# A hybrid decoder step on one core: the second token group's queries without their norm, routes among the dots, kept weights, and other last groups

## The reference

```python
h = h + merged @ w_out                                   # after three gated branches
x = _rmsnorm(h, norm2_g)                                 # h * rsqrt(mean(h*h) + 1e-6) * g
q = (x @ w_q).reshape(t, 8, 2, 128)                      # 8 product-key heads
s = einsum('thpc,pkc->thpk', q, sub_keys)                # scores against 2 x 128 keys
sv, si = top_k(s, 16); cand = sv[..0..] + sv[..1..]      # 256 candidates of a head
cv, ci = top_k(cand, 16); experts = i1 * 128 + i2        # 16 of 16384 experts
act = gelu(einsum('thkd,td->thk', u_tab[experts], x))    # dots with the first table
h = h + einsum('thk,thkd->td', softmax(cv) * act, v_tab[experts])
y = _rmsnorm(h, final_norm_g)
```

## Time and profile before

| | |
|---|---|
| median of three runs | 1943.35 us (1941.68 to 1944.21) |
| profiled execution | 1947.41 us, of it span 1945.6 us |
| PE, DVE, ACT, POOL busy | 86%, 71%, 27%, 34% |
| granted TensorE clock, mean | 0.949 |
| DMA | 675.14 MB, of which 577.23 MB are gathers |

### The profile page before, as it was taken

How to read it: one execution, slowest core, us unless ns; L and a number is a source line. 1 busy time by engine, 2 the same in 40 slices (tenths; PEclk the granted TensorE clock), 3 DMA queues, 4 the chain that set the end, 5 groups by cost and what they waited for, 6 DMA issues and landing times.

```text
span 1945.6 us, 17733 instructions
## 1 busy us (share of the span) xinstructions
PE 1674.4 (86%) x5411; PEld 999.5 (51%) x5411; DVE 1388.4 (71%) x3407; ACT 521.7 (27%) x1203; POOL 663.9 (34%) x605
## 2 busy tenths in 40 slices
PE   8999999999888999998868999877777777787876
PEld 7888987887555555554434555323333212333332
DVE  5998684227788777777787778776777776777754
ACT  3121142113333433332222223332222122321221
POOL 0020030002434343333434344444444453445441
PEclk9999999999999999999979999998999898989898
DMA  5452465548999999999989999999999999999995
GB/s 209 141 87 98 154 146 164 176 150 339 418 400 412 419 418 418 418 419 401 419 349 413 419 420 414 421 422 410 414 419 413 412 416 419 408 414 415 421 412 245
DMA packets 112687, 675.14 MB, mean 347 GB/s; under 512 B 12784, under 2 KB 15296, under 8 KB 42576
## 3 DMA queue, kind: packets, MB, share of 16 engines
q0 software_dynamic: 80816, 577.23, 73.0%
q1 hardware_dynamic: 31216, 95.87, 14.3%
q10 hardware_dynamic: 560, 0.92, 0.2%
HBM read 665.79 MB, written 6.21 MB: 345 GB/s over the span
## 4 chain that ended last, share of the span: by engine, by line
PE 46%; DMA 36%; issue 8%; DVE 6%; POOL 2%; ACT 2%; ACTq 0%; DVEq 0%; POOLq 0%
DMA upper<-in_peer_uv,upper 20%; PE pair L1157 19%; DMA lower<-in_peer_uv,upper 16%; PE pair L667 7%; PE pair L678 6%; PE pair L1024 4%; DVE upper L2080 2%; PE pair L781 2%; ACT upper L1550 1%; PE pair L972 1%; POOL upper L643 1%; DVE lower L2080 1%; POOL lower L643 1%; PE pair L793 1%; PE pair L712 1%
## 5 line engine op out<-in xcount | busy, mean ns | idle before, releaser
L1157 PE MATMUL pair<-upper 128*128 128x512 f32 (+1 forms) x1144 | 570.4, 641 | 152.6 <-ACT upper L1550 152.3
L643 POOL DMA_INDIRECT upper<-in_peer_uv,upper x324 | 369.2, 1139 | 500.6 <-PE pair L1157 437.4
L1157 PE MATMUL pair<-lower,upper 128*128 128x512 f32 (+1 forms) x772 | 382.1, 637 | 93.7 <-ACT upper L1550 93.6
L1157 PEld LDWEIGHTS pair<-upper 128*128 128x128 f32 (+1 forms) x1144 | 218.5, 198 | 434.0 <-issue 276.0
L643 POOL DMA_INDIRECT lower<-in_peer_uv,upper x220 | 255.2, 1160 | 483.0 <-PE pair L1157 305.0
L2080 DVE CUSTOM_DVE_ANT_0 upper<-upper 128x1024 f32<-128x1024 f32 x172 | 210.7, 1225 | 122.4 <-DMA upper<-in_peer_uv,upper 122.1
L1157 PEld LDWEIGHTS pair<-lower,upper 128*128 128x128 f32 (+1 forms) x772 | 148.0, 198 | 283.5 <-issue 185.5
L2080 DVE CUSTOM_DVE_ANT_0 upper<-upper,lower 128x1024 f32<-128x1024 f32 x152 | 185.8, 1222 | 87.6 <-DMA upper<-in_peer_uv,upper 86.7
L1550 ACT ACTIVATE upper<-upper 128x128 f32<-128x128 f32 (+1 forms) x479 | 159.9, 386 | 308.3 <-DVE upper L2096 308.1
L2080 DVE CUSTOM_DVE_ANT_0 lower<-lower,upper 128x1024 f32<-128x1024 f32 x116 | 142.1, 1225 | 85.5 <-DMA lower<-in_peer_uv,upper 85.5
L1024 PE MATMUL pair<-lower 128*128 128x288 f32 x704 | 194.0, 413 | 2.6 <-ACT upper L1420 2.6
(11 more groups left out here) (420 smaller groups left out, 1760.6 us busy)
## 6 DMA issues: line engine op xcount, KB each, us to landing
lower<-in_w_in SPq DMA_DIRECT2D x64, 512.0 KB, 7.0
lower<-in_peer_q SPq DMA_DIRECT2D x32, 512.0 KB, 7.9
lower<-in_proj SPq DMA_DIRECT2D x48, 256.0 KB, 7.1
lower<-in_w_out SPq DMA_DIRECT2D x16, 512.0 KB, 6.0
upper<-in_peer_uv,upper POOLq DMA_INDIRECT x324, 11.8
upper<-in_cache_k SPq DMA_DIRECT2D x8, 512.0 KB, 4.5
upper<-in_cache_v SPq DMA_DIRECT2D x8, 512.0 KB, 3.7
lower<-in_peer_uv,upper POOLq DMA_INDIRECT x220, 11.8
```

The costliest lines, as they stand in the source:

```text
L643: pool.indirect_dma_start(row(g), None, a["peer_uv"], bass.IndirectOffsetOnAxis(ap=idx[:, n % 8, j:j + 1], axis=0)).then_inc(row_in[g % RI ...
L1157: mm = pe.matmul(pairs[n % 2][0:rows, h, :], diag[:, (nth - 1) % DIAGS, 0:rows], row(g)[:, D + h * 512:D + (h + 1) * 512], start=(j == min ...
```

## The change

Five edits. (1) The second group's `xbT_b` is h g2 without the norm's factor, written by DVE behind each w job. The sums of squares are taken as columns (job sq, 24 narrow matmuls), and the factor `rcol_b` (three columns) multiplies the scores in ACT's copies out of PSUM and the argument of the gelu. The queries of head 0 start before the sums, and the transposes of h are split around them; empty slots are 4 + 4 in place of 15 + 6. (2) Route 1 is no longer ahead of the first dot: routes 1 and 2 run in job 0, five steps behind each dot from the fifth on. ACT's exponentials follow. (3) Three heads' first parts, in place of four, are ahead of the loop. (4) The query weights of heads 1 and 2 (four blocks of 512 KB) get a place of their own in the memory of ring places 8 and 9, are loaded once the trunk no longer needs it, and gathers 8 and 9 wait until they have been used. (5) The last job's groups are 4, 4, 2 and six single rows, in place of 4, 4, 4 and four single ones; the residual is added in PSUM before row 13, in place of row 12.

```diff
-EARLY_HEADS = 4
+EARLY_HEADS = 3
...
-BANK_JOBS += [("gapm", 8)] + [(f"w{_j}", KD) for _j in range(KD)] + [("gap0", 15), ("ssb", KD)]
-for _t in range(2, 5):
-    BANK_JOBS += [(f"ht{_t}.{_b}", 4) for _b in range(2)] + [(f"gaph{_t}", 2)]
-BANK_JOBS += [("q0.0", KD), ("q0.1", KD)] + [(f"xt{_t}.{_b}", 4) for _t in range(2, 5) for _b in range(2)]
+BANK_JOBS += [("gapm", 8)] + [(f"w{_j}", KD) for _j in range(KD)] + [("gap0", 4)]
+BANK_JOBS += [(f"ht{_t}.0", 4) for _t in range(2, 5)] + [("q0.0", KD), ("q0.1", KD), ("sq", KD)]
+BANK_JOBS += [(f"ht{_t}.1", 4) for _t in range(2, 5)] + [("gaph", 4)]
+BANK_JOBS += [(f"xt{_t}.{_b}", 4) for _t in range(2, 5) for _b in range(2)]
...
+KEPT = ["Aq1.0", "Aq1.1", "Aq2.0", "Aq2.1"]
...
-    last = [range(12, 16)] if n < NJ - 1 else [range(j, j + 1) for j in range(12, 16)]
-    return [range(0, 4), range(4, 8), range(8, 12)] + last
+    ends = (4, 8, 12, 16) if n < NJ - 1 else (4, 8, 10, 11, 12, 13, 14, 15, 16)
+    return [range(lo, hi) for lo, hi in zip((0,) + ends, ends)]
...
+        kept_w = at(33024, 4, 1024)
...
+            def kept_loads():
+
+                sp.wait_ge(lnx_ok, 2 * HALF - 1)
+                for i in range(4):
+                    sp.dma_start(kept_w[:, i, :], a["peer_q"][2 + i]).then_inc(kept_in[i], 16)
+
             for h in range(PH):
+                if h == 1:
+                    kept_loads()
                 for b in range(2):
-                    late_load(f"Aq{h}.{b}", a["peer_q"][2 * h + b])
+                    if f"Aq{h}.{b}" not in KEPT:
+                        late_load(f"Aq{h}.{b}", a["peer_q"][2 * h + b])
...
+                if g in (8, 9):
+                    bank_filled(pool, f"Aq{g - 7}.1")
...
+            def late_squares():
+
+                ps = begin_bank("sq")
+                pe.wait_ge(h2sqb_ok, KD)
+                n = 0
+                for t in range(3):
+                    for k in range(KD):
+                        mm = pe.matmul(ps[:, 4 * t:4 * t + 4], h2sq_b[:, k, t * P:(t + 1) * P], ones[:, 0:4],
+                                       start=(k == 0), stop=(k == KD - 1))
...
-                for _ in range(15):
+                for _ in range(4):
                     yield
-                ps = begin_bank("ssb")
-                for k in range(KD):
-                    pe.wait_ge(h2sqb_ok, k + 1)
-                    mm = pe.matmul(ps[:, 0:REST], ones, h2sq_b[:, k, :], start=(k == 0), stop=(k == KD - 1))
...
+                for t in range(2, 5):
+                    yield from turned(f"ht{t}.0", h2T_b, t, P if t < TILES else NB * NT, 4)
+                for b in range(2):
+                    yield from dense_query(0, b)
+                yield from late_squares()
+                for t in range(2, 5):
+                    yield from turned(f"ht{t}.1", h2T_b, t, P if t < TILES else NB * NT, KD)
...
-                    if n == NJ - 1 and j == 12:
+                    if n == NJ - 1 and j == 13:
...
-                               scale=rcol[:, t:t + 1] if t < 2 else 1.0).then_inc(gel_ok, 1)
+                               scale=rcol[:, t:t + 1] if t < 2 else rcol_b[:, t - 2:t - 1]).then_inc(gel_ok, 1)
...
+            act.wait_ge(rcol_ok, 3)
+            exp_of(0)
             first_query(1)
-            for h in range(1, EARLY_HEADS):
-                first_query(h + 1)
-                if h == 1:
-                    act.wait_ge(rcol_ok, 3)
-                first_score(h)
-                if h != 2:
-                    exp_of(h // 2)
+            first_query(2)
+            first_score(1)
...
+                yield GROUP - 1
+                for h in range(2, EARLY_HEADS):
+                    first_query(h + 1)
+                    first_score(h)
...
-                    act.activation(h2sq_b[:, j, :], h2T_b[:, j, :], ACT.Square).then_inc(h2sqb_ok, 1)
+                    act.activation(h2sq_b[:, j, 0:REST], h2T_b[:, j, :], ACT.Square)
+                    act.activation(h2sq_b[:, j, REST:].rearrange("p (r t) -> p r t", r=3),
+                                   h2T_b[:, j, FIRST:].unsqueeze(1).to_broadcast([P, 3, 32]), ACT.Square
+                                   ).then_inc(h2sqb_ok, 1)
...
-                        act.activation(sc(16 + h)[:, b, :], ps[:, 0:P], ACT.Copy)
+                        act.activation(sc(16 + h)[:, b, :], ps[:, 0:P], ACT.Copy, scale=rcol_b[:, 0:1])
...
-                if j == 2 and 2 <= n + 1 < NJ:
+                if j == (2 if n else 7) and n + 1 < NJ:
                     exp_of(n + 1)
...
+                    bank_emptied(dve, f"w{j}")
+                    ts(xbT_b[:, j, 0:REST], h2T_b[:, j, :], c("g2", j), None, ALU.mult)
+                    ts(xbT_b[:, j, REST:].rearrange("p (r t) -> p r t", r=3),
+                       h2T_b[:, j, FIRST:].unsqueeze(1).to_broadcast([P, 3, 32]), c("g2", j), None, ALU.mult
+                       ).then_inc(xbTb_ok, 1)
+                yield PLACE["sq"] + 8
+                ps = bank_filled(dve, "sq")
...
+                yield PLACE["sq"] + 10
                 dve.wait_ge(h2rb_ok, 1)
-                link(dve.reciprocal(h2r_b, h2r_b))
-                for k in range(KD):
-                    made = after(stt(xbT_b[:, k, 0:REST], h2T_b[:, k, :], c("g2", k), h2r_b, ALU.mult, ALU.mult))
...
+                dve.reciprocal(rcol_b, rcol_b).then_inc(rcolb_ok, 1)
...
-            for n in range(1, LAG):
-                for _ in route(n):
-                    pass
...
-            gates(0)
+
+            def first_routes():
+
+                for n in range(1, LAG + 1):
+                    yield from route(n)
...
-                ways = route(n + LAG) if n + LAG < NJ else iter(())
+                ways = first_routes() if n == 0 else route(n + LAG) if n + LAG < NJ else iter(())
                 for j in range(TOPK):
                     dot(n, j)
                     k = 4 * n + j // GROUP
-                    if j % GROUP == 0 and k:
+                    if j % GROUP == 0 and k and (n < NJ - 1 or j <= 8):
                         weigh(k - 1)
-                    if n == NJ - 1 and j >= 12:
+                    if n < NJ - 1 or j < 8:
+                        if j % GROUP == 1 and k:
+                            add_group(k - 1)
+                    elif j == GROUPS[GROUP_OF[n, j]][1][-1]:
                         weigh(GROUP_OF[n, j])
-                    elif j % GROUP == 1 and k:
-                        add_group(k - 1)
-                    for _ in range(2):
+                    if n == 0 and j == GROUP - 1:
+                        gates(0)
+                    for _ in range(2 if n else 5 if j >= GROUP else 0):
                         next(ways, None)
```

86 lines of the change are left out of this document (42 added, 44 removed).

## The result

The changed kernel takes **1933.19 us**, the median of five runs (1932.41 to 1937.21), beside 1944.21 (1941.68 to 1946.05) for the kernel before on the same chip: a ratio of 0.9948, with an interval from 0.9935 to 0.9962. The change gains 10 us, where 20.3 were forecast; 1933.2 lies above the range of 1917 to 1931. The profiled execution took 1937.21 us (span 1935.4) against 1947.41 before, also 10.2 less. The runs that follow ran on several chips, whose kernel before took 1943.5 to 1946.3 us, so kernels are compared by their ratios to the kernel before on the same chip, not by their microseconds. Where two ratios are compared, the uncertainty given is the 95% one of their difference. One execution of 5922.52 us, of the kernel without the kept blocks, is left out of that kernel's median and ratio as disturbed.

The account below looks back on a forecast made before the run. The DMA stream, fed through ten ring places, was taken to set the pace. Gains of 5.0 + 2.4 + 7.5 + 5.4 = 20.3 us from 1943.35 gave 1923.1 us, range 1917 to 1931.

Parts of the forecast that it names:

- What bounds the kernel: Expert part: DMA's stream at 421 GB/s sets the pace; time is its start, bytes, dry stretches and the tail.
- a stall in a place where the trace of before has none: Anywhere in the trace: listed among the signs that would show the prediction wrong; no size given.
- 13 empty slots fewer: Second group's norm, before the queries: lets the transposes start earlier; no gain or cost booked.
- The first job: Start of the stream: 5.0 us for four blocks less and 2.4 us for the dip from 480 to 490.
- The 5.0 for the bytes: Start of the stream: four weight blocks less beside the gathers, 1.25 us each, gain 5.0 us.
- No gap: Start: first ring place back near 465, while rows 0 to 9 and two blocks keep DMA busy until 473.
- Case 1: Rival on the first job: DVE limits it, 7.4 us given back, 1930.5, chance 0.12; sign: DMA windows under 400 GB/s, 470-510.
- The norm: Second group's norm, slice 21's dip: removing DVE's block between two dots gains 7.5 us.
- case 2: Rival at the norm: a wait for the root or sq halves the gain; 1926.9, up to 1930; chance 0.12.
- case 3: Rival at the norm: new DVE scalings lock GpSimd's descriptor writes, costing 5.2 us; 1928.3; chance 0.04.
- The end: Last job's groups: PE runs without rest and ends at 1932.7 in place of 1938.1, gain 5.4 us.
- case 4: Rival at the end: PE's clock falls again, last groups gain only 2.5 us; 1926.0; chance 0.10.

Follow-up runs that it names:

- two slots in the changed kernel: The changed kernel with a job of two empty slots behind head 3's scores: 1930.54 us, ratio 0.9924.
- two slots in the start part: The start part with two empty slots behind head 3's scores: 1935.38 us, ratio 0.9953 to the kernel before.
- start part: The kernel before with edits 2 to 4 of the change alone, old norm and last groups: 1941.7 us, ratio 0.9985.
- four rows against five: The changed kernel with eleven empty slots behind head 3's scores, against thirteen: 1931.63 us, ratio 0.9941, against 1926.89 us, ratio 0.9916.
- all nine kernels: Kernels with the whole change, kept blocks and routes in job 0: mean ratio 0.9943 for four with g0.0 in a group's last row, 0.9922 for five in its first.
- Moving the gates and projections by one row: The changed kernel with two of the eight empty slots ahead of w0 moved ahead of g0.0: 1932.01 us, ratio 0.9923.
- four early heads: The changed kernel with four heads' first parts ahead of the loop in place of three: 1930.69 us, ratio 0.9923.
- slots and copies together: The changed kernel with two empty slots and ACT's copies of the late heads never behind the next group's gelu: 1928.75 us, ratio 0.9922.
- moving what lies behind the gates alone: The changed kernel with ten in place of eight empty slots ahead of w0, only later jobs one row later: 1935.53 us, ratio 0.9943.
- the run of the norm alone: The kernel before with edit 1 of the change alone: 1938.4 us, ratio 0.9971.
- five rows later: The changed kernel with thirteen empty slots behind head 3's scores: 1926.89 us, ratio 0.9916.
- no kept blocks: The changed kernel with the four weight blocks of heads 1 and 2 loaded into the ring again: 1939.64 us, ratio 0.9973.

## Why the prediction was wrong

**What bounds the kernel: right.** The large gains and losses of this study can be read as DMA run dry or as bytes, or as the tail behind the last row, though one trace of each kernel does not find every microsecond of the ratios again. But each edit was priced as if the jobs between stood still.

**The step that failed** is the one that has no number in the prediction: "a stall in a place where the trace of before has none" stood in the list of what would make it wrong, and this is what came. EARLY_HEADS was costed at its 7.07 us of queries ahead of the loop, and "13 empty slots fewer" in the norm's part, but that these move each later job against the groups of four was not costed at all. It costs 4.7, 6.2 and 4.9 us in three pairs (two slots in the changed kernel, two slots in the start part, four rows against five), 4.2 over all nine kernels. Moving the gates and projections by one row gives 4.9, with an uncertainty of 3.7. That the place costs this in kernels with the change is shown; it is no fixed price, for in the kernel before the same shift cost nothing in sum. The mechanism (PE stands with a job's first matmul ahead of a whole group's matmuls, for a bank that ACT frees only behind that group's gelu and diagonals) is read from the timelines and borne out by the table, in which no kernel of the first kind waits under 3.5 us and none of the second over 2.6. It is a little under half of the missing ten.

**The first job: the sum within what was measured, the parts wrong.** 5.0 + 2.4 = 7.4 were forecast. Well placed, the start part gives 9.1 (6.2 to 12.1) in the kernel before, of which 5.4 stand in the old norm's stretch and some is lost again behind it. Beside the new norm and end it gives 6.2 (uncertainty 3.9): 0.9923 with four early heads against the 0.9955 that the other two parts make if added. The 5.0 for the bytes holds with the routes in job 0 (4.9), and is nothing that could be measured without them (0.8, -1.9 to 3.5). The prediction had seen that the blocks filled the time ahead of the eleventh gather, and drew from it that the early places were no gain; it follows just as much that the blocks are none by themselves. The two terms are one: fewer blocks pay only with the earlier place. Whether the earlier place pays without the kept blocks was not run. The "No gap" of the prediction did not hold in full: in the changed kernel's windows the dip went from 480-490 (321) to 490-500 (350), and 440 to 500 loses 6.0 us in place of 7.6, 1.6 of the 2.4. Case 1, DVE as the limit of job 0, did not come at its size: the windows 480 to 510 hold 420, 350 and 406 GB/s. But one window is under 400, its own sign, with DVE busy for 9.79 and 9.26 us of the ten from 480 and from 490, so a small part of it may be there.

**The norm: right, size over.** 7.5 were forecast, 5.6 (3.9 to 7.4) measured alone. The mechanism is as told: the block is gone and its windows are full; the difference lies outside them. In the changed kernel 4.1 us are left in 970 to 1030, so case 2 came in part, not through sq's wait, but through ACT's squares and a table load ahead of a gelu. In the runs with better places this loss is mostly 1.0 to 2.0 us, but 4.4 in the run with slots and copies together and 4.0 in the start part with the old norm and slots; moving what lies behind the gates alone gave the 1.0 us above. What of the norm's remainder belongs to its place is left open.

**The port rule (case 3): no cost seen.** GpSimd's issue at 994.55 takes its usual 0.94 us with a scaling of 96 columns beside it at 994.57, and what GpSimd had waited for was PE. Issues of up to 1.97 us stand where no scaling is beside them (1003.62). One scaling took longer than its 0.37 us, inside an issue of 1.76 us that had begun at 968.25; which of the two held the other, if either did, the rows don't tell:

```profile
968.25 1.76 POOL L657 DMA_INDIRECT lower<-in_peer_uv,upper  x1 [0.73 <-issue]
969.61 0.53 DVE L2197 TENSOR_SCALAR lower<-upper 128x288 f32<-128x288 f32 x1
```

By this, the rule of the Trainium skill (SBUF — State Buffer, on the shared port pair) cost nothing that these rows show; in the run of the norm alone the stream lost nothing at all from 970 to 1030.

**The end: mechanism right, term too large.** 5.4 forecast, 3.1 measured alone, 4.4 in the two profiles. PE runs through without a pause. The term was read from one profile whose clock was in the dear case. The prediction saw that clock (0.54) and feared it for the changed kernel, case 4; it was the number of before that stood at the dear end of its spread.

**The sum.** Measured one by one: start part well placed 9.1, norm 5.6, end 3.1, together 17.8; with all of it and the places of before 14.8 to 15.0 are measured (two slots, four early heads). The difference of some 3 us is within what the intervals add up to. It also has a reason that the windows show: the start part alone already takes 5.4 us off the old norm's stretch, and the norm's part alone takes the same stretch to nothing, so that the sum of the two counts some of it twice. From the forecast's 20.3, take 2.3 for the end and 1.9 for the norm, add 1.7 for the start: 17.8. Take 2.9 that the parts do not give together and 4.8 for the places: 10.1, the gain that was measured.

## What to carry to other kernels

A step that moves a hand-placed schedule can have a price of its own, apart from what it adds or removes: count out, from the kernel's list of jobs, in which row of a group each later job begins, before and after, and look above all for jobs whose first instruction stands ahead of a whole group in one engine's order and waits for a resource that another engine frees behind that group. If such a job exists, two empty slots can be worth as much as an edit of the arithmetic; here 0.9924 (two slots) and 0.9916 [0.99, 0.9932] (thirteen) against 0.9948 for the change as it was. And a long wait in a list is a cost only if nothing would have been waited for in its place: 5.0 us at the attention had covered most of a wait of 4.55 us for the next diagonal, while loads that "only cost bytes" may be filling a time in which the stream had nothing else to move.

## What was not expected of the hardware

With the same last groups the end of the kernel comes in a few sizes, and TensorE's granted clock tells which: from the last dot to the last sum about 5.3 or 7.05 us with the new groups, 8.4, 10.05 or 11.5 with the old ones. PE's sixteen pieces take 7.13 us at the full clock and 10.13 where it was partly the lower. In the changed kernel the first eight pieces behind a pause of 2.75 us took 5.39 us at a granted clock of 0.66 (1905 to 1910); with five rows later, the gates later and no kept blocks they took 3.70 behind a pause of 2.73 or 2.74. So the length of the pause alone does not say which size comes. A term read from a stretch at the lower clock should be taken with the same stretch at the full one beside it.
